# Expert weights fetched in release order, some through reused places outside the ring, in 16 KB rows, with half-row ranking

## The reference

```
def expert_choice_moe(h, router_w, wg, wu, wd):
    cap = CAPACITY_FACTOR * n // N_EXPERTS                  # 64
    aff = jax.nn.softmax((h @ router_w).astype(jnp.float32), axis=-1)
    gate, idx = lax.top_k(aff.swapaxes(1, 2), cap)          # per expert, over 512 tokens
    xs = jax.vmap(lambda hb, ib: hb[ib])(h, idx)
    a = jnp.einsum('becd,edf->becf', xs, wg)
    u = jnp.einsum('becd,edf->becf', xs, wu)
    y = jnp.einsum('becf,efd->becd', jax.nn.silu(a) * u, wd) * gate[..., None]
    return zeros(n, d).at[idx].add(y)
```

## Time and profile before

| | |
|---|---|
| Median of 3 runs | 1594.43 us (1590.89 to 1596.54) |
| Profiled execution | 1598.6 us, its span 1597.0 us, granted TensorE clock 0.974 |
| PE busy | 1441.7 us, 90% of the span |
| DVE, ACT busy | 433.9 us and 230.0 us |
| DMA | 501.39 MB, mean 314 GB/s |
| Chain that ended last | PE 57%, DMA 35%, DVE 5% |
| SP waiting to issue an expert granule until PE is done with a slot | 789.5 us in 174 waits |

### The profile page before, as it was taken

How to read it: one execution, slowest core, us unless ns; L and a number is a source line. 1 busy time by engine, 2 the same in 40 slices (tenths; PEclk the granted TensorE clock), 3 DMA queues, 4 the chain that set the end, 5 groups by cost and what they waited for, 6 DMA issues and landing times.

```text
span 1597.0 us, 15305 instructions
## 1 busy us (share of the span) xinstructions
PE 1441.7 (90%) x5897; PEld 593.9 (37%) x5897; DVE 433.9 (27%) x851; ACT 230.0 (14%) x469; POOL 71.1 (4%) x151
## 2 busy tenths in 40 slices
PE   4997999997999999898889999996999998898996
PEld 2553555553433332232323444453433322323322
DVE  2113567334021121121112332535112111111113
ACT  3223333111101010010002111220100101000001
POOL 1000000000000000000000300000000000000001
PEclk9999999998999999999999999997999999999999
DMA  9729652029999999999999202207899999999995
GB/s 349 283 105 369 224 211 106 14 101 412 420 421 421 421 421 422 421 422 422 421 422 386 92 0 106 104 27 291 354 386 421 421 421 422 422 422 421 421 421 211
DMA packets 95345, 501.39 MB, mean 314 GB/s; under 512 B 7560, under 2 KB 8607, under 8 KB 46014
## 3 DMA queue, kind: packets, MB, share of 16 engines
q1 hardware_dynamic: 88064, 485.22, 74.8%
q0 software_dynamic: 2304, 8.39, 1.4%
q10 hardware_dynamic: 4926, 7.04, 1.2%
HBM read 494.32 MB, written 6.31 MB: 313 GB/s over the span
## 4 chain that ended last, share of the span: by engine, by line
PE 57%; DMA 35%; DVE 5%; issue 1%; ACT 1%; ACTq 1%; POOL 0%; POOLq 0%; DVEq 0%; SPq 0%
PE PS L986 20%; DMA ring<-in_exp_wd_dram 17%; DMA ring<-in_exp_wu_dram 16%; PE PS L780 7%; PE PS L698 4%; PE PS L647 3%; PE PS L812 3%; PE PS L617 3%; PE PS L1000 3%; PE PS L854 2%; PE PS L629 2%; PE PS L654 1%; PE PS L875 1%; PE PS L795 1%; DMA ring<-in_ada_w_dram 1%
## 5 line engine op out<-in xcount | busy, mean ns | idle before, releaser
L986 PE MATMUL PS<-ring,arena 128*64 128x512 f32 x2976 | 674.3, 600 | 55.4 <-DMA ring<-in_exp_wg_dram 19.6
L986 PEld LDWEIGHTS PS<-ring,arena 128*64 128x64 f32 x2976 | 216.0, 137 | 495.0 <-issue 370.6
L1648 DVE TENSOR_TENSOR x<-x,PS 128x512 f32<-128x512 f32 x128 | 87.9, 687 | 471.7 <-PE PS L1000 471.7
L1000 PE MATMUL PS<-arena 128*128 128x512 f32 x256 | 141.5, 641 | 3.7 <-DVE arena L1675 3.2
L780 PE MATMUL PS<-ring,hT 128*128 128x512 f32 x256 | 115.0, 605 | 0.0
L1294 ACT ACTIVATE arena<-PS 128x512 f32<-128x512 f32 x32 | 17.4, 594 | 469.0 <-PE PS L986 469.0
L1675 DVE SCALAR_TENSOR_TENSOR arena<-PS,arena,g_row 128x512 f32<-128x512 f32 x32 | 22.6, 746 | 227.5 <-PE PS L986 227.5
L1000 PEld LDWEIGHTS PS<-arena 128*128 128x128 f32 x256 | 38.3, 188 | 105.1 <-issue 96.9
L617 PE MATMUL PS<-ident,arena 128*128 128x128 f32 (+5 forms) x393 | 54.3, 278 | 24.4 <-DVE arena L1666 18.0
L629 PE MATMUL PS<-ring,cond 128*32 128x512 f32 x384 | 52.8, 683 | 21.3 <-DMA ring<-in_ada_w_dram 20.7
L780 PEld LDWEIGHTS PS<-ring,hT 128*128 128x128 f32 x256 | 49.2, 194 | 61.0 <-issue 61.0
(11 more groups left out here) (172 smaller groups left out, 1020.6 us busy)
## 6 DMA issues: line engine op xcount, KB each, us to landing
ring<-in_exp_wg_dram SPq DMA_DIRECT2D x64, 2048.0 KB, 22.8
ring<-in_exp_wd_dram SPq DMA_DIRECT2D x62, 2048.0 KB, 26.1
ring<-in_exp_wu_dram SPq DMA_DIRECT2D x60, 2048.0 KB, 25.9
ring<-in_ada_w_dram SPq DMA_DIRECT2D x24, 2048.0 KB, 11.8
ring<-in_conv_w_pw_dram SPq DMA_DIRECT2D x6, 2048.0 KB, 20.5
ring<-in_mix_w_out_dram SPq DMA_DIRECT2D x2, 2048.0 KB, 10.0
xn_rows<-xn ACTq DMA_DIRECT2D x8, 512.0 KB, 4.7
arena<-in_exp_wu_dram SPq DMA_DIRECT2D x2, 2048.0 KB, 21.0
```

Source lines behind the costliest of these rows:

```text
L986: last = nc.tensor.matmul(PS[64 * e:64 * e + 64, bank + half, :], lhs[:, k, 64 * e:64 * e + 64], w[e][kk][:, half * N:(half + 1) * N], sta ...
L1000: nc.tensor.matmul(PS[:, 6 + i % 2, :], hot[:, (i // 2) * 128:(i // 2 + 1) * 128], y_rows[:, (i % 2) * N:(i % 2 + 1) * N], start=True, sto ...
L1648: v.tensor_tensor(part, part, PS[:, 6 + i % 2, :], ALU.add).then_inc(scat_added, 1)
```

## The change

1. **Order of SP.** `mix_w_out` is loaded behind the late conditioning blocks, with all of `ada` 20 to 23 behind it.
2. **First granules by release time.** Layer 0 loads 6, 0, 1, 7, 2, 3, 4, 5, 8, and layer 1 loads 0, 1, 2, 3, 6, 4, 5, 7, 8.
3. **Places outside the ring used twice.** Granules 15, 16 and 17 go to the three places again, each when 6, 7 or 8 was used.
4. **16 KB rows.** A granule is now half the rows of a matrix for one expert: one row of 16 KB for each partition. Two granules belong together, PE starts when both are there, and both count as used together. The old cut (`by_quarters`) stays for the first two granules of a layer and for its last pair.
5. **Column halves.** `mix_w_out` and `pw2` are cut by columns, in rows of 2 KB (before 4 KB): a half of the product needs one granule, and the first granule's slot is free after the last product of half 0.
6. **Half-row ranking.** The affinities stand as 32 rows of 256 (tokens 0 to 255 on partitions 0 to 15, the rest on 32 to 47). Each half is ranked to its best 64, and the two descending lists are merged by taking the larger of entry i of one and entry 63 - i of the other. The transposes of the first half go ahead of the last tile (`affT` 0).
7. **Less filler.** `keep_warm` at the start of the mixture 10 to 6 in layer 0, before `slotT` in layer 1 4 to 2; the last tile of xn is saved before `affT` instead of behind it.

```
+SPARE = ((SLOTS, SLOTS + 1, SLOTS + 2), (15, 16, 17))
+SPARED = SPARE[0] + SPARE[1]
+FIRST_LOADS = ((6, 0, 1, 7, 2, 3, 4, 5, 8), (0, 1, 2, 3, 6, 4, 5, 7, 8))
+def by_quarters(j, q):
+    return isinstance(j, int) and ((j == 0 and q < 2) or j == PAIRS - 1)
...
+                if by_quarters(j, q):
+                    sp.dma_start(dst.rearrange("p (e n) -> p e n", e=2),
+                                 src[j, :, :, 2 * D * (q % 4):2 * D * (q % 4 + 1)]).then_inc(arrived, 16)
                     return
-                sp.dma_start(dst.rearrange("p (e n) -> p e n", e=2),
-                             src[j, :, :, 2 * D * (q % 4):2 * D * (q % 4 + 1)]).then_inc(arrived, 16)
+                rows = src[j, :, q % 2, 4 * D * (q // 2 % 2):4 * D * (q // 2 % 2 + 1)]
+                if dst is not None:
+                    sp.dma_start(dst, rows).then_inc(arrived, 16)
+                    return
...
+                for n in FIRST_LOADS[l]:
+                    if n in SPARE[0]:
+                        spare_free(l, SPARE[0].index(n))
+                        load_spare(l, n, SPARE[0].index(n))
+                    else:
+                        load_slot(l, n)
+                for n in range(len(FIRST_LOADS[l]), 24):
+                    if n in SPARE[1]:
+                        i = SPARE[1].index(n)
+                        sp.wait_ge(moe_used, MOE_GRANULES * l + SPARE[0][i] + 1)
+                        load_spare(l, n, i)
+                    else:
+                        load_slot(l, n)
...
                 t, half = ITEMS[n][1]
-                wait_granule(G_MIXOUT)
-                wait_granule(G_MIXOUT + 1)
+                wait_granule(G_MIXOUT + half)
...
+                for q in range(q0, q0 + 4, 2):
+                    if by_quarters(j, q):
...
+                    w = arrived(l, j, q), arrived(l, j, q + 1)
+                    for kk in range(4):
+                        last = one_row(2 * (q - q0) + kk, (w[0][kk], w[1][kk]), lhs, bank)
+                        if kk == 3:
+                            last.then_inc(moe_used, 2)
+                        if scattering is not None and kk % 2:
+                            scatter_part(scattering, q + kk // 2)
...
             def mixture(l):
-                keep_warm(6 if l else 10)
+                keep_warm(6)
...
-                src = affT[0:EXPERTS, :]
+                src = affT[0:LISTS, :]
...
+                v.tensor_tensor(take, far_best[0:EXPERTS, :], near_best, ALU.is_gt).then_inc(v_chain, 1)
+                v.tensor_scalar(far, best_at[32:LISTS, ::-1], float(N // 2), None, ALU.add).then_inc(v_chain, 1)
+                v.tensor_copy(to, near_at).then_inc(v_chain, 1)
+                v.tensor_tensor(gates[0:EXPERTS, :], far_best[0:EXPERTS, :], near_best, ALU.max).then_inc(v_chain, 1)
+                chain.n += 4
+                dve.wait_ge(v_chain, chain.n)
+                chain(v.tensor_tensor(far, far, to, ALU.subtract))
+                chain(v.tensor_tensor(far, far, take, ALU.mult))
+                v.tensor_tensor(to, to, far, ALU.add).then_inc(slots_ready, 1)
```

More of the change, by code:

```diff
@@ L211 @@
          + [("ada", b) for b in range(2 * (EARLY + LATE), 2 * SECTIONS)]
-         + [("moe0", n) for n in range(12 * PAIRS) if n not in SPARE]
+         + [("moe0", n) for n in range(12 * PAIRS) if n not in SPARED]
          + [("pw1", q) for q in range(4)] + [("pw2", 0), ("pw2", 1)]
-         + [("moe1", n) for n in range(12 * PAIRS) if n not in SPARE])
+         + [("moe1", n) for n in range(12 * PAIRS) if n not in SPARED])
 GRANULE = {name: g for g, name in enumerate(ORDER)}
@@ L522, in _, with load_granule @@
                 sp.dma_start(late_slot(b), ada_blocks(0)[EARLY, b, :, :, :]).then_inc(slot_in[(G_LATE + b) % SLOTS], 16)
-            for h in range(2):
-                g = G_MIXOUT + h
-                load(g, [(slot(g).rearrange("p (k n) -> p k n", k=4),
-                          mix_w_out[0, h * N:(h + 1) * N, :].rearrange("(k p) n -> p k n", p=128))])
-            def load_quarter(l, j, q, dst, arrived):
+            def load_granule(l, j, q, dst, arrived):
                 w = (exp_wg, exp_wu, exp_wd)[q // 4]
@@ L558, in load_pair @@
[L558 to L568 removed]
+                    g = GRANULE[(f"moe{l}", 24 + q)]
@@ L578, in _ @@
                       .then_inc(slot_in[(G_LATE + b) % SLOTS], 16)
-            for b in range(2 * SECTIONS - 2, 2 * SECTIONS):
+            for h in range(2):
+                g = G_MIXOUT + h
+                load(g, [(slot(g).rearrange("p (k n) -> p k n", k=K8),
+                          mix_w_out[0, :, h * N:(h + 1) * N].rearrange("(k p) n -> p k n", p=128))])
+            for b in range(2 * (EARLY + LATE), 2 * SECTIONS):
                 load_ada(b)
-            load_pair(0, 0)
-            load_pair(0, 1)
-            with sp.Fori(2, PAIRS, 1) as j:
+            load_first_pairs(0)
+            with sp.Fori(2, PAIRS - 1, 1) as j:
                 load_pair(0, j)
+            for n in range(12 * (PAIRS - 1), MOE_GRANULES):
+                load_slot(0, n)
             sp.dma_start(tab, nc.inline_tensor(conv_tables(), "conv_tables").ap()).then_inc(tables_in, 16)
-            sp.wait_ge(moe_used, SPARE[2] + 1)
+            sp.wait_ge(moe_used, SPARE[1][2] + 1)
             sp.dma_start(dw_rows[0:CONVW, :], w_dw[0, :, :]).then_inc(tables_in, 16)
@@ L597, in _ @@
                 g = G_PW2 + h
-                load(g, [(slot(g).rearrange("p (k n) -> p k n", k=4),
-                          pw2[0, h * N:(h + 1) * N, :].rearrange("(k p) n -> p k n", p=128))])
+                load(g, [(slot(g).rearrange("p (k n) -> p k n", k=K8),
+                          pw2[0, :, h * N:(h + 1) * N].rearrange("(k p) n -> p k n", p=128))])
             sp.dma_start(bias_row, b_pw2[0, :].unsqueeze(0).to_broadcast([128, D])).then_inc(bias_in, 16)
-            load_pair(1, 0)
-            load_pair(1, 1)
-            with sp.Fori(2, PAIRS, 1) as j:
+            load_first_pairs(1)
+            with sp.Fori(2, PAIRS - 1, 1) as j:
                 load_pair(1, j)
+            for n in range(12 * (PAIRS - 1), MOE_GRANULES):
+                load_slot(1, n)
             for t in range(T):
@@ L755, in fill @@
                 elif kind == "affT":
-                    pe.wait_ge(aff_ready, T * (1 + l))
-                    for t in range(T):
-                        last = transpose(B[0:EXPERTS, t * 128:(t + 1) * 128], aff[:, t, :])
+                    pe.wait_ge(aff_ready, T * l + 2 * args[0] + 2)
+                    for i in range(2):
+                        last = transpose(B[0:EXPERTS, i * 128:(i + 1) * 128], aff[:, 2 * args[0] + i, :])
                 elif kind == "slotT":
@@ new lines, in arrived @@
+            def arrived(l, j, q):
+                if isinstance(j, int) and 12 * j + q in SPARED:
+                    i = SPARED.index(12 * j + q) % 3
+                    pe.wait_ge(spare_in[i], (16, 16, 48)[i] * (2 * l + j + 1))
+                    if i == 2:
+                        return [spare_parts[0][:, 0:D], spare_parts[0][:, D:2 * D], *spare_parts[1:3]]
+                    rows = spare[i]
+                elif isinstance(j, int):
+                    n = GRANULE[(f"moe{l}", 12 * j + q)]
+                    wait_granule(n)
+                    rows = slot(n)
+                else:
+                    n = GRANULE[(f"moe{l}", 24 + q)]
+                    pe.wait_ge(slot_in[n % SLOTS], j * 32 + (arrivals(n) - 64))
+                    rows = slot(n)
+                return [rows[:, i * D:(i + 1) * D] for i in range(4)]
```

158 lines of the change are left out of this document (74 added, 84 removed).

## The result

| | before | after |
|---|---|---|
| Median | 1594.6 us of 4 runs (1590.9 to 1596.5) | 1570.6 us of 4 runs (1568.0 to 1573.8) |
| Ratio | | 0.9853, 95% interval 0.9827 to 0.9879 |
| Profiled execution, span | 1598.6 us, 1597.0 us | 1571.0 us, 1569.2 us |

The time fell by 24.0 us, to 1570.6; 1570 was forecast, from 1556 to 1583. The two spans differ by 27.8 us, more than the medians: the profiled execution of before, 1598.6 us, is longer than each of its four timed runs.

The account below looks back on a forecast made before the run. The prediction took the DMA expert stream to bound both mixtures and PE to bound the rest. Its terms, -7.0 - 7.6 - 4.0 - 2.8 + 8 - 10.6, sum to -24.0 us: 1570 us from the median 1594.4, range 1556 to 1583.

Parts of the forecast that it names:

- Term 1: Attention, head 1: with mix_w_out behind the late blocks, the wait for a conditioning block goes, -7.0 us.
- Term 2: Start of layer 0's mixture: two granules load earlier, ranking is shorter, first release 3.5 us earlier, small new holes; -7.6 us.
- Term 3: Start of layer 1's mixture: shorter ranking gives 5.4 us, colder PE costs 1 to 2; -4.0 us.
- Term 4: Stream holes: the one at granule 15 closes in layer 1, -2.8 us; new ones from granule 24, +4 us each layer.
- Term 5: Expert rows of 16 KB: a line through the 2 KB and 8 KB rates gives 427 GB/s, -5.3 us each layer.
- Term 6: Remaining parts, such as pw2's column halves and the 3.65 us tail after the last landing: nothing on the path.
- the sign of a falling clock in `wd`: Mixtures: the prediction called itself wrong if PE's clock falls in wd; no size given.
- row size counts: Expert stream: the rival said row size does nothing and the rate stays at 421 GB/s; 1581 us, chance 0.18.
- 433 GB/s was not reached: Expert stream: the rival said long rows reach 433 GB/s or more; 1561 us, chance 0.17.
- Pairs did cost: Mixtures: the rival said PE idles longer in wd and starts cold, +5 us each layer; 1580 us, chance 0.12.

Follow-up runs that it names:

- e1: The kernel before with only mix_w_out and all of ada 20 to 23 loaded behind the late conditioning blocks: 1587.55 us, ratio 0.9954.
- e9: The changed kernel itself, run again in a later series: 1568.1 us, ratio 0.9834.
- e3: The changed kernel, still releasing by twos, with each 16 KB row fetched as two of 8 KB and the first pair's wg in the old cut: 1575.87 us, 0.9880.
- e4: The changed kernel with each 16 KB row fetched as four of 4 KB and the first pair's wg in the old cut: 1596.76 us, ratio 1.0018.
- e2: The changed kernel with the old cut for every expert granule, 8 KB rows, each released by itself: ratio 0.9865.

## Why the prediction was right, step by step

**Term 1** (mix_w_out, -7.0): head 1 is 8.0 us shorter, and alone it gives 7.4. The slow block went with the stall, as assumed.

**Term 2** (start of layer 0, -7.6). The mechanism was right and its pieces were off against one another. PE's start moved by 12.2 us with term 1, 0.3 more than forecast, but that is luck: 9.9 of it are in e1, and 2.3 are left where 4.9 stood. `slotT` did come earlier as said, by 4.7 us against e1 (363.71 and 368.38, 4.1 forecast). The filler was sized at 8.4 us and took 8.49; what was missed is the wait for rows behind it, 4.22 us, because the gather took 11.9 us beside the longer rows instead of the 9.3 of e1. The latency of 1.5 us in this term stood on no row either: the arena's granule, alone in the queue, took 7.2 us from issue to landing, 2.3 more than the 4.91 of its bytes. The first hole was put at 1.6 us and is (427 - 158) / 427 x 5 = 3.1 us. The first release came 5.5 us behind the first product (387.15 and 381.62), where 3.5 was taken, because the first granules ran cold (clock 0.50 in the window at 380 us, which is 1.2 GHz, after a wait of 4.22 us), which the sum left out. The conv mark moved by 18.2 us. Without term 1 (8.0), with the holes behind (+3.0) and the rate (-4.8), 8.4 us are left for this term.

**Term 3** (start of layer 1, -4.0): about right, though the two profiles first read make it look under-sized. From the conv mark to the first product it is 252.3 us instead of 258.9, which is 6.6. DVE's ranking runs from 1096.38 to 1113.26 us before and from 1074.71 to 1087.08 after: 4.5 us shorter, and the copy ahead of it wins 0.6. That is 5.1 where 5.4 stood, the merge being dearer than 1.2: its instructions take 0.18 to 0.21 us, one behind another. The length of one instruction was right: 0.420, 0.410 and 0.401 us. The cold filler costs 7.28 instead of 5.42, 1.9 us, inside the 1 to 2 forecast. The rest of the 6.6 us lies ahead of it: the last router product ran cold before, 3.57 us, and takes 2.10 now, and the convolution before it is 1.4 us shorter. The products are the same ones. The code of e1 is that of before here; the last router product in before and in e1:

```profile
1089.44 3.57 PE L753 MATMUL PS<-router,hT 128*128 128x16 f32 x16 [1.27 <-DVE hT L1480]
...
1079.94 2.08 PE L750 MATMUL PS<-router,hT 128*128 128x16 f32 x16 [1.27 <-DVE hT L1477]
```

So the 3.57 belong to that one execution and not to the change. From the conv mark to the first product e1 takes 256.2 us, and against it the changed kernel won 3.9 us (252.3) and 4.4 (251.8 in e9): the 4.0 of the forecast.

**Term 4** (holes, -2.8 and +8): none at 15, and one before 24 in both layers, with the second dip 12 us later that was put at 11 or 26. Layer 0 loses 3.0 us and layer 1, with (109 + 60 + 224) / 427 x 5, 4.6 us (1180 to 1185 us runs at 367 GB/s), against 4 each. In e9, with 272, 408 and 351 GB/s in the same three windows of layer 1, it is 2.9 us.

**Term 5** (rows, -10.6): 427 and 428 GB/s, as the line says; 4.8 us a layer at these rates against 5.3, because the rate before was 422 in these windows and not 421. The term was right in the rate and not in what it is worth: about 1 us in layer 0 and 3.4 to 6.0 in layer 1 came through (e3), the rest went into the first hole and the later rows. A slip in its sum did no harm: 387 and 421 GB/s give 9.1 ns fixed, not 8.3, beside the 36.9 ns per 1000 B. The rule of the Trainium skill, "DMA: Bandwidth & Descriptors", section Specifications, that was weighed there would have left this term out. e4 shows it plainly: rows of 4 KB cost 26 us over rows of 16 KB. In the long windows the rate stayed below the ceiling that the same section puts at 435 GB/s.

**Term 6** (nothing): the filler of layer 1 was the exception, and it was counted in term 3. The tail was another. From the landing of the last expert load to the end of the span it is 24.0 us, before 22.3 (22.8 in e9). PE ran cold in `wd` of layer 1's last pair, with the clock at 0.66 from 1530 to 1540 us, and was behind the stream there:

```profile
1534.70 16.11 PE L1017 MATMUL PS<-ring,arena 128*64 128x512 f32 x64 [0.73 <-issue]
```

The same 64 instructions take 13.95 us in `wd` of an earlier pair (at 703.53 us). So the sign of a falling clock in `wd`, by which the prediction called itself wrong, did show in this one place, for 0.6 to 1.8 us.

The rivals: row size counts (0.18 given to it), 433 GB/s was not reached (0.17). Pairs did cost (0.12 given): e2 and e3 put it at about 1 us in layer 0 and up to 3.6 in layer 1, not 5. They showed in the hole before 24, which the forecast had, and in the clock of the long windows, 0.98 against 1.00. There it fell not in `wd` but behind PE's wait for the first granules of the next pair, 2.79 us before 660.78 us, where the granule took 5.35 us instead of 3.65. The forecast's sum is good to 1 us partly by luck. Layer 1's start looks 2.6 us better and the mixture of layer 1 (-2.8 against -4.1) worse, and e1 and e9 put both down to the one execution of each kernel that was read. In layer 0 a dearer gather, cold first granules and a larger first hole stood against a `slotT` that was earlier than said. And the span of before lay 4 us above its median, so the marks moved by 27.6 us for a change of 24.0.

## What to carry to other kernels

Find which side holds a stream in each stretch, and count its idle places in bytes not moved: early loads, extra places and longer rows each moved or made a hole elsewhere here, and taking one of them back cost 2 to 7 us where 24 came of all. Fetch in long rows where the stream is the bound, but look at the small transfers beside it that PE waits for, and release buffers one by one where the ring is short of free slots; both at once, by granule, had the lowest median (1.8 us below its neighbour, which is not clear of the noise). Look at what stands in front of a small block that the compute engine needs soon: four granules put behind it were worth 7 us, a third of the change, in one move of a few lines. And read a stage of a few us from two executions: one product that ran cold in a single profile made a term of 4 us look like 6.6.

## What the hardware showed

- A DMA engine's time for a row fits 9.1 ns and 36.9 ns per 1000 B within 1 GB/s over the whole span tried: 387 to 388, 410, 422 and 427 to 428 GB/s at 2, 4, 8 and 16 KB, at full share each time.
- The first gather of 0.52 MB beside the stream took 11.9 us from issue to landing with rows of 16 KB in the stream, 9.5 with 8 KB and 8.5 with 4 KB.
- `MAX8`, `FIND_INDEX8` and `MATCH_REPLACE8` take 0.68, 0.67 and 0.66 us on 512 elements and 0.42, 0.41 and 0.40 on 256, so by the line through both about 0.15 us are fixed, which is also the time of the smallest DVE instruction (0.154). If 48 partitions in place of 16 added anything, it is inside that; the two were not changed one by one.
- PE came out of a wait of 4.22 us at clock 0.50, and its first release came 5.5 us behind its first product. Before, where the filler ran up to the products and the clock was 1.00, it came 3.7 us behind (393.81 to 397.50).
